# A two-layer encoder on one core: layer 0's input projection, local attention and convolution taps rebuilt, output weights loaded in earlier stages

## The reference, cut to what matters

```python
# layer 0 mixer
h = x @ w_in                                   # 1024 -> u 512, gate 512, q 512, k 128, v 128
h = u * sigmoid(gate)                          # depthwise conv, 31 taps, centred, plus bias
conv_out = silu(layer_norm(conv(h), g, beta))
q, k = rotate the first 16 of 64 columns of each head
s = q.k * 64**-0.5, masked to |kpos - qpos| <= 128     # 8 heads, 2 key-value heads
m = max(max(s), sink); p = exp(s - m); p = p / (sum(p) + exp(sink - m))
mix = concat([conv_out, p @ v]) @ w_out
# layer 1 mixer: full attention, 16 heads, 4 key-value heads, @ w_out
x = layer_norm(ALPHA * x + mix)                # then 16 experts, each takes its top rows
x = layer_norm(ALPHA * x + experts(x))
```

## Time and profile before

| | us |
|---|---|
| median of 3 runs | 4053.07 (4053.01 to 4056.72) |
| the profiled execution | 4054.61 |
| its span, first to last instruction | 4052.8 |
| its mean granted TensorE clock | 0.932 of 2.4 GHz |
| busy: TensorE, VectorE, ScalarE, GpSimd | 3559.1, 2558.3, 2051.5, 589.4 |

### The profile page before, as it was taken

The page is one execution under the profiler, slowest core; times in us unless marked ns, Lnnn a source line. Parts: engine busy times, 40 slices in busy tenths (PEclk is TensorE's granted clock), DMA queues, the critical chain, the costliest instruction groups (busy, mean ns, idle before and its releaser), DMA issues. The chain is left out here.

```text
span 4052.8 us, 55505 instructions
## 1 busy us (share of the span) xinstructions
PE 3559.1 (88%) x19780; PEld 2878.7 (71%) x19780; DVE 2558.3 (63%) x3835; ACT 2051.5 (51%) x2785; POOL 589.4 (15%) x540
## 2 busy tenths in 40 slices
PE   8997676693999999998799689997976999999993
PEld 7885554483999999997355345554856999999993
DVE  1115997456676667665465568885556766676665
ACT  1113554322666666664133578885223666666664
POOL 0003775001011111110011000000001111111102
PEclk9998777795999999999899899998988999999997
DMA  2100000324778778774321100002245777787774
GB/s 108 32 24 30 14 18 1 115 111 149 258 238 253 240 247 256 241 250 120 149 83 68 58 26 26 21 21 63 104 151 179 249 248 247 239 257 247 248 234 153
DMA packets 359325, 585.25 MB, mean 144 GB/s; under 512 B 17216, under 2 KB 283456, under 8 KB 357696
## 3 DMA queue, kind: packets, MB, share of 16 engines
q1 hardware_dynamic: 332800, 486.52, 35.9%
q0 software_dynamic: 14336, 50.34, 5.6%
q10 hardware_dynamic: 12096, 47.19, 2.9%
HBM read 505.36 MB, written 78.64 MB: 144 GB/s over the span
## 5 line engine op out<-in xcount | busy, mean ns | idle before, releaser
L1083 PE MATMUL h_ps<-xT,high 128*128 128x384 f32 x3584 | 1066.2, 360 | 2.8 <-DVE xT L1205 2.8
L1201 DVE TENSOR_TENSOR low<-raw,high 128x2048 fp32r<-128x2048 f32 x384 | 877.1, 2285 | 147.9 <-ACT high L1145 147.9
L1084 PE MATMUL h_ps<-xT,low 128*128 128x192 f32 x3584 | 905.4, 253 | 0.0
L1145 ACT ACTIVATE high<-raw 128x2048 fp32r<-128x2048 f32 x384 | 732.8, 1909 | 282.9 <-PE yp_ps L1116 176.1
L1084 PEld LDWEIGHTS h_ps<-xT,low 128*128 128x128 f32 x3584 | 684.7, 191 | 1.3
L1083 PEld LDWEIGHTS h_ps<-xT,high 128*128 128x128 f32 x3584 | 675.7, 189 | 4.9 <-issue 3.4
L1272 DVE TENSOR_TENSOR gate_up<-h_ps,cross 128x384 f32<-128x384 f32 x256 | 142.9, 558 | 309.1 <-ACT cross L1164 307.8
L407 POOL TENSOR_TENSOR conv<-conv,product 128x497 f32<-128x497 f32 (+14 forms) x240 | 243.5, 1050 | 437.7 <-ACT product L575 437.7
L1008 POOL TENSOR_TENSOR still<-still 128x1 f32<-128x1 f32 x96 | 25.8, 269 | 1659.9 <-DVE work L1289 1298.6
L1164 ACT ACTIVATE cross<-h_ps 128x384 f32<-128x384 f32 x256 | 125.4, 490 | 279.0 <-PE h_ps L1087 278.8
L1408 PE MATMUL qkv_ps<-w_in,xT 128*128 128x512 f32 x576 | 254.7, 598 | 9.5 <-ACT xT L1428 6.9
(11 more groups left out here) (220 smaller groups left out, 6419.1 us busy)
## 6 DMA issues: line engine op xcount, KB each, us to landing
raw<-moe_w_gate SPq DMA_DIRECT2D x128, 1024.0 KB, 5.8
raw<-moe_w_up SPq DMA_DIRECT2D x128, 1024.0 KB, 8.2
raw<-moe_w_down SPq DMA_DIRECT2D x128, 1024.0 KB, 8.6
rows_x<-x ACTq DMA_DIRECT2D x36, 512.0 KB, 2.6
x<-x SPq DMA_DIRECT2D x24, 512.0 KB, 3.5
rows_acc<-ax ACTq DMA_DIRECT2D x24, 512.0 KB, 2.9
r<-rows_acc SPq DMA_DIRECT2D x24, 512.0 KB, 7.6
rows_qT_parts<-qT ACTq DMA_DIRECT2D x12, 1024.0 KB, 3.9
```

The source lines that it names most:

```text
L1083: nc.tensor.matmul(ps, wh[:, n, k, :], xT[:, u, k, :, :].rearrange("p s n -> p (s n)"), start=(k == 0), stop=False)
L1084: nc.tensor.matmul(ps[:, 0:SLOTS], wl[:, n, k, :], xT[:, u, k, 0, :], start=False, stop=False)
L1145: nc.scalar.activation(split_view(high, at), piece_view(at), ACT.Copy).then_inc(high_ready, 1)
L1201: nc.vector.tensor_tensor(split_view(low, at), piece_view(at), split_view(high, at).bitcast(F32), ALU.subtract).then_inc(low_ready, 1)
```

## The change

It replaces the bodies of `project_conv_window` and `window_and_taps` and changes where w_out is loaded.

- **Projection.** The weights come in eight chunks of the qkv columns and eight of the u and gate columns, are rounded by ScalarE and subtracted by VectorE, and x likewise; every product is now three fp32r products, and u and gate too have tokens on partitions. `glu` of a tile is therefore transposed by TensorE (one tile later) and copied by ScalarE. k needs one place for both heads. ScalarE makes the copies of q, k and v that VectorE made. All loops over tiles are written out. From tile 4 on VectorE does taps between its other work: 12 behind tile 4's glu, then 12 ahead of and 12 behind the glu of each tile 5 to 11, that is all 124 of the 512 prompt columns and 14 for each channel group of columns 512 to 1008.
- **Attention and taps.** A unit is now four heads, two of each key-value head: q's 128 partitions hold a pair of heads, one for each, and score products take 64 partitions. The probabilities are scaled by ScalarE before they are transposed, and the product with the values has channels on partitions, so that the output needs no scaling and no transposing. GpSimd and ScalarE do no taps; VectorE does all that are left (248 operations), spread over the units by size. `conv` is the first half of `cat`. At its end SP loads all eight chunks of layer 0's w_out.
- **project_out** gets `early`, views of raw chunks already in SBUF: 8 in layer 0, 3 in layer 1 (loaded in `axial_attention` where the prompt's keys are no longer read). The late five of layer 1 have a buffer each, among them buffers that the stage uses later. The tables stand behind them.

```diff
@@ project_conv_window
+            @block.sync
...
+                for k in range(KD):
+                    sp.dma_start(raw_qkv[:, k, :], win[:, k, kv_cols]).then_inc(qkv_in[k], 16)
+                load(1)
...
+                    if k < 6:
+
+                        sp.wait_ge(qkv_low, min(KD, ((k + 1) * UG - 1) // CHUNK + 1))
+                    else:
+                        sp.wait_ge(ug_low, k - 5)
+                    sp.dma_start(raw_ug[:, k % 6, :], win[:, k, ug_cols]).then_inc(ug_in[k], 16)
...
+            @block.tensor
...
+                def product(t, out, at, parts, arrived):
+                    for k in range(KD):
+                        if t == 0:
+                            pe.wait_ge(arrived, k + 1)
+                        cols = slice(k * P, (k + 1) * P)
+                        for n, (one, other) in enumerate(((xh, wh), (xh, wl), (xl, wh))):
+                            for lo, hi in parts:
+                                last = nc.tensor.matmul(out[:, lo:hi], one[:, t % 2, cols], other[:, k, at + lo:at + hi],
...
+                for t in range(TILES):
+                    pe.wait_ge(xl_ready, t + 1)
+                    if t:
+                        pe.wait_ge(copied, t)
+                    product(t, qkv_ps, UG, ((0, WIN_Q),), qkv_low)
+                    if t:
+                        pe.wait_ge(k_ready, t)
+                    product(t, qkv_ps, UG, ((WIN_Q, CHUNK),), qkv_low).then_inc(qkv_done, 1)
+                    if t + 1 < TILES:
+                        turn_x(t + 1)
+                    if t:
+                        turn_glu(t - 1)
+                    product(t, ug_ps, 0, ((0, CONV), (CONV, UG)), ug_low).then_inc(ug_done, 1)
+                    pe.wait_ge(rotated, t + 1)
...
+            @block.vector
...
+                for t in range(TILES):
+                    rotate(t)
+                    if t + 1 < TILES:
+                        low_x(t + 1)
...
+                    if t > GROUP_TILES[0]:
+                        convolve(STEP_TAPS // 2, GROUP_TILES[0] if done[0] + STEP_TAPS // 2 <= len(prompt) else 2 * GROUP_TILES[0])
+                    v.wait_ge(sig_ready, t + 1)
+                    nc.vector.tensor_tensor(sig[:], ug_ps[:, 0:CONV], sig[:], ALU.mult).then_inc(gl_ready, 1)
+                    if t >= GROUP_TILES[0]:
+                        convolve(STEP_TAPS // 2, GROUP_TILES[0] if done[0] + STEP_TAPS // 2 <= len(prompt) else 2 * GROUP_TILES[0])
@@ window_and_taps, TensorE
+                def qk(n):
...
+                    for j in range(2):
+                        for kv in range(WIN_KV):
+                            rows, h = slice(DH * kv, DH * (kv + 1)), 2 * kv + j
+                            last = nc.tensor.matmul(s_ps[:, h * HALF:h * HALF + NK], q[rows, t % RING, (2 * part + j) * P:(2 * part + j + 1) * P],
+                                                    keys[rows, t * P:t * P + NK], start=True, stop=True)
...
+                def pv(n):
...
+                    for k in range(3):
+                        for kv in range(WIN_KV):
+                            last = nc.tensor.matmul(o_ps[DH * kv:DH * (kv + 1), part * 2 * P:(part + 1) * 2 * P], values[:, t + k, kv * DH:(kv + 1) * DH],
+                                                    pT[:, n % 2, (k * G + 2 * kv) * P:(k * G + 2 * kv + 2) * P], start=(k == 0), stop=(k == 2))
...
+                qk(0)
+                for n in range(UNITS):
+                    if n + 1 < UNITS:
+                        qk(n + 1)
+                    turn(n)
+                    if n:
+                        pv(n - 1)
+                pv(UNITS - 1)
@@ window_and_taps, VectorE
+                for ct in range(CT):
+                    for at in range(TAPS):
+                        todo += [(ct, at, part) for part in (SECOND_SPLIT if at < SOON_TAPS else (FIRST_PART, SECOND_PART))]
...
+                soft(0)
+                convolve(0.02)
+                invert(0)
+                for n in range(UNITS):
+                    if n + 1 < UNITS:
+                        soft(n + 1)
+                    copy(n)
+                    convolve(0.02 + 0.98 * (n + NEAR) / UNITS)
+                    if n + 1 < UNITS:
+                        invert(n + 1)
+                    convolve(0.02 + 0.98 * (n + FAR) / UNITS)
@@ window_and_taps, ScalarE
+                for n in range(UNITS):
+                    copy(n)
+                    if n + 1 < UNITS:
+                        exps(n + 1)
+                        norm(n + 1)
+                    if n % 2 == 0 and n:
+                        out(n // 2 - 1)
@@ project_out
+        late = [] if EARLY == KD else [raw[:, 0, :], raw[:, 1, :], x1[:, 0, :], x1[:, 1, :], ax1[:, 0, :], ax1[:, 1, :], row[:], xT[:]]
...
-                for k in range(KD):
-                    if k >= 2:
-                        sp.wait_ge(w_low, k - 1)
...
+                for k in range(EARLY, KD):
+                    for side, rows in enumerate(out_weight_rows(m, layer, k)):
+                        sp.dma_start(raw_weight(k)[DH * side:DH * (side + 1), :], rows).then_inc(w_in[k], 16)
+                load(Tile(0, 0))
...
                 for k in range(KD):
                     v.wait_ge(w_high, k + 1)
+                    if k and EARLY:
+                        v.wait_ge(w_low, k)
@@ axial_attention, SP
+                with sp.Fori(GROUP_TILES[0], GROUP_TILES[0] + 2) as t:
+                    load(t)
+
+                sp.wait_ge(scores, number(GROUP_TILES[0], 0, 2 * SET))
+                for k in range(len(early)):
+                    for side, rows in enumerate(out_weight_rows(m, 1, k)):
+                        sp.dma_start(early[k][DH * side:DH * (side + 1)], rows.rearrange("p (j n) -> p j n", j=2)).then_inc(weights_in, 16)
+                with sp.Fori(GROUP_TILES[0] + 2, TILES) as t:
+                    load(t)
+                sp.wait_ge(weights_in, 32 * len(early))
```

More of the change, by code:

```diff
@@ new lines, in convolve @@
+                def convolve(count, ready):
+                    v.wait_ge(glu_ready, ready)
+                    for ct, at, part in todo[done[0]:done[0] + count]:
+                        if at:
+                            v.wait_ge(tapped, done[0] - CT + 1)
+                        tap(nc, conv, glu, taps, conv_b, ct, at, part).then_inc(tapped, 1)
+                        done[0] += 1
+                for at in (slice(0, P), slice((TILES + 1) * P, (TILES + 2) * P)):
+                    s.add(nc.vector.memset(keys[:, at], 0.0))
@@ L339, in window_and_taps @@
+                assert done[0] == len(todo), (done[0], len(todo))
+def window_and_taps(c, m, keys, values, glu, cat, taps, conv_b, early):
     nc = c.nc
@@ L553, in _, with convolve @@
-                turns(s.loop(CT - 1, UNITS * 4), turn)
+                done = [0]
+                todo = []
+                for ct in range(CT):
+                    for at in range(TAPS):
+                        todo += [(ct, at, part) for part in (SECOND_SPLIT if at < SOON_TAPS else (FIRST_PART, SECOND_PART))]
+                size = [part[1] - part[0] + 50 for _, _, part in todo]
+                total = sum(size)
+                def convolve(share):
+                    while done[0] < len(todo) and sum(size[:done[0] + 1]) <= total * share + 1:
+                        ct, at, part = todo[done[0]]
+                        if done[0] >= 2:
+                            v.wait_ge(tapped, done[0] - 1)
+                        tap(nc, conv, glu, taps, conv_b, ct, at, part).then_inc(tapped, 1)
+                        done[0] += 1
@@ L614, in norm_channels @@
+                exps(0)
+                norm(0)
+                for n in range(UNITS):
[5 more added lines that the diff above has]
+                        out(n // 2 - 1)
+                out(TILES - 1)
 def norm_channels(c, m, acc, cat):
```

663 lines of the change are left out of this document (306 added, 357 removed).

## The result

| | before | after |
|---|---|---|
| median of 4 runs, us | 4053.53 (4053.01 to 4056.72) | 3835.61 (3833.49 to 3838.31) |
| ratio of the times | | 0.9461, 95% interval 0.9445 to 0.9478 |
| span of the profiled execution | 4052.8 | 3831.7 |

The change takes 218 us off, 5.4%. The forecast was 3850.0 (3826 to 3892).

The account below looks back on a forecast made before the run. TensorE was taken to bound the projection, VectorE attention and taps, chunk loading the output projections' start. From 4053.07, -52.5 - 107 - 23 - 21 = -203.5 gives 3849.6, forecast 3850 us (3826 to 3892).

Parts of the forecast that it names:

- Which limit rules which stage: Three stages, three limits: TensorE in the projection, VectorE in attention and taps, waiting for weight chunks at the output projections' start.
- The projection, -52.5: Layer 0's projection: 21.6 us a tile instead of 26.2, taps hidden except 7.8 at the end; 280 instead of 332.65.
- The attention stage, -107: Attention and taps: VectorE's work sets 9.4 us a unit instead of 13.8; stage 243 instead of 349.8.
- 9.2 to 9.6: Attention stage: the period in us that would show the forecast right, with VectorE busy over 90%.
- Taps with GpSimd idle: VectorE's taps: columns/960 + 0.13 us each, 0.56 for 416 columns, against 0.98 while GpSimd adds.
- The score products in pairs, 0.75: Attention stage: two score products on different row halves overlap, 0.75 us a pair, against 0.66 each by the 0.437.
- A: Attention stage: row halves don't overlap, clock stays lower, TensorE and the chain bound it; +48, 3898; chance 0.12.
- Output projections, -23 and -21: Start of layer 0's and layer 1's output projections: early or at-once weights bring the first sum sooner, -23 and -21.
- B: VectorE sets the projection's period through dearer operations, +31, and attention grows by as much as 50; 3931; chance 0.05.
- D: Projection: split products run at half clock, 43 us a tile, +238, net +34; 4088; chance 0.01.
- E: Output projections: weights' loads are hidden already, so they lose nothing; +44, 3894; chance 0.02.
- C: Lower ends hold: no 0.13 between VectorE taps that don't wait, no stall per unit; 3820 to 3830; chance 0.1.

Follow-up runs that it names:

- e5_one_f32_product: Changed kernel with one float32 product of the rounded parts in place of three fp32r products in the projection; 3888.97 us, ratio 0.9588.
- e3_taps_all_later: Changed kernel with no taps in the projection, all done by VectorE in the attention stage; 3933.38 us, ratio 0.9708.
- e1_late_at_once: Changed kernel with no output weight loaded in an earlier stage, all eight chunks issued at once in project_out; 3854.74 us, ratio 0.9515.
- e2_old_ring: Changed kernel with the old loading of output weights: two buffers, none loaded early, tables behind the second chunk; 3880.94 us, ratio 0.9578.
- e6_before_no_gpsimd: Kernel before, without GpSimd's adds and the ScalarE products feeding them (30 of 31 taps of columns 0 to 704 left out); 3977.15 us, ratio 0.9809.
- e7_gpsimd_adds: Changed kernel with 160 GpSimd adds of 497 columns on an unread buffer in the attention stage; 3960.99 us, ratio 0.9773.
- e4_same_half: Changed kernel with attention products on one half of the array issued in a row instead of alternating; 3832.23 us, ratio 0.9461.
- e9_taps_sooner: Changed kernel with taps begun at tile 2, moving 24 more operations of 496 columns out of the attention stage; 3825.54 us, ratio 0.9441.
- e10_both: Changed kernel with taps begun at tile 2 and ScalarE making the whole copy of the turned probabilities; 3827.49 us, ratio 0.9443.

## Why the prediction held, step by step

- **Which limit rules which stage**: right in all three stages. The projection went with the product's price alone (e5_one_f32_product), the attention stage with VectorE's work (e3_taps_all_later), the output projections with the arrival of chunks (e1_late_at_once, e2_old_ring).
- **The projection, -52.5**: measured -53.1. The period was 21.45 for 21.6, since 256 columns cost 0.117 and not the 0.13 taken; half of the price of 512 was the right end. The first tile was over at 35.0, not 33.7, which takes back most of what the shorter period gave. A tap cost 0.645 for some 490 columns, and the taps were hidden. The bare taps at the end were there, 7.78 us; without them the stage would end only 5.8 sooner, because the last tile's turn and copy of glu then stand bare in their place.
- **The attention stage, -107**: mechanism right, size 10 us short (232.4 for 243), and the period of 8.94 lies below the 9.2 to 9.6 that were named as its sign. The term that was off is VectorE's small work per unit, put at 3.65: measured are masks and small operations 2.38, copy 0.60 and sum with reciprocal 0.28, together 3.26, or 9 us in 23 periods. 23 times (9.4 - 8.94) are 10.6 us, the whole of the error; the beginning (first copy 19.4 after the start, not 20.8) and the end (7.4, not 6.2) cancel. Two more errors cancel within the periods. The sum spread all taps over 24 units and then added 6.2 for the last ones once more; in the trace 7 taps (2.7 us) stand ahead of the first copy and 9 (6.0 us) behind the last. Against that, VectorE waited for turns for 6.8 us in the 23 periods and not for 2.3: 0.2 to 0.75 in each of six units whose turns took 2.2 to 2.8 us, 3.65 in all, and 3.15 ahead of the last copy, where it has no masks left to do. The 0.2 that was taken for turns at half clock was thus about the average, but it comes unevenly.
- **Taps with GpSimd idle**: the step that carries most of the gain, and right. The price of 416/960 + 0.13 was read from ten taps in one idle stretch; e6_before_no_gpsimd gives 0.573 (137.5/240) over all 240 operations, and with adds on GpSimd alone (e7_gpsimd_adds) the high price is there again. What the prediction did not see is how steep the contention is: it took 0.98 with adds beside for the cost, but that was an average over taps with and without an add in front; adds without a pause make it 1.57.
- **The score products in pairs, 0.75**: the price was right, 0.78 (1.57 for four), the reason is not shown. It was taken because two column halves overlap; e4_same_half has the same 1.57 with the products of one row half one behind the other, and why a product on 64 rows costs 0.39 and not 0.66 stays open. In that the price was lucky. The granted clock was 0.83 in the stage, so rival **A** did not come about. But its chain is close, an estimated 0.7 us a unit behind. The Trainium skill (TensorE: Matmul & The Clock Gate, Part 3) would have given an estimated 0.66 a pair; the trace shows 0.78, and by e4_same_half the order of the two halves doesn't decide it.
- **Output projections, -23 and -21**: measured -24.2 and -21.3; the first sums came at 19.6 for 21 and 24.4 for 24. In layer 1 chunks land 2.15 us apart, as taken. The tables behind them, called "just in time", are 2.3 us late for VectorE, but ahead of the second tile's low part, where it costs nothing.
- **B, D and E** are excluded by the period of 21.45, the clock of 1.00 in the projection, and the two stages' gains. **C**, all lower ends together, would have been 3820 to 3830; the result, 3835.6, lies in the lower part of the own case's 3830 to 3872: the 0.13 between taps and some of the stalls did not vanish.
- Some 5 us of the span's 221 lie in stages that were not changed. Two profiles of the changed kernel differ by 2.9 there, and all the experiments spread over 2904.6 to 2910.6 with 2909.7 for the kernel before, so nothing shows that these 5 us belong to the change.

## What to carry to other kernels

A second engine that shares the work can cost more than it does: before work is split between VectorE and GpSimd, compare the durations of the same VectorE operation with GpSimd busy and idle in the same trace, the small operations too, and price the split by the difference. When work is moved off an engine that sets a stage, look at the next chain in the same unit (here the ScalarE copy's wait for the turns), since its length caps the gain. Where loads are late behind a ring of buffers, first issue them all at once: that alone gave 28 us here, and the 19 of loading sooner need room in an earlier stage.

## What the runs showed of the hardware

- A tap on VectorE (two inputs in SBUF) and a GpSimd add took turns, one for one: 1.57 us a tap of 496 columns instead of 0.645, and up to 1.20 instead of 0.16 for four columns. Operations that read PSUM were untouched (0.55 and 0.68). 160 adds of no use cost the kernel 125 us, 0.78 each.
- Float32 score products of 64 rows and 384 columns took 0.39 us each at full clock (four in 1.57), alternating between the two row halves as well as two after another on the same half. Products with 64 output columns did lose overlap when the same half was issued in a row (51.7 to 59.4 us in all).
- TensorE's granted clock in the attention stage was 0.83 with the engine busy 60% of the time, and it went up and down within the stage: twelve turns took 1.53 us in one unit and 2.81 in the next. In e9_taps_sooner and e10_both the stretch from 330 to 430 was granted 0.91 and 0.90 instead of 0.85, but over the whole stage it was 0.84 and 0.82, as good as the same.
- The subtractions of the low parts, with weights in place, ran 1.33 us apart; the transfers of two times 64 partitions brought a chunk of 0.52 MB every 2.15 to 2.19 us, some 240 GB/s, and in layer 1's output projection ScalarE waited for each of the last chunks, the last of them at 13.4 of the 24.4 us to the first sum.
